# Two decoder stacks in one kernel: sums of squares taken as the residual is added, first weight splits moved ahead of the norm's transposes, separate last sums, and decay-mixer heads taken in pairs

## What is computed

```python
def rms_norm(x, g, eps=NORM_EPS):
    xf = x.astype(jnp.float32)
    y = xf * lax.rsqrt(jnp.mean(xf * xf, axis=-1, keepdims=True) + eps)
    return (y * g.astype(jnp.float32)).astype(x.dtype)

def swiglu_ffn(h, norm, w13, w2):
    u = rms_norm(h, norm) @ w13
    return (jax.nn.silu(u[..., :FFN_HIDDEN]) * u[..., FFN_HIDDEN:]) @ w2

def wkv7_scan(r, w, k, v, a, bb):          # the decay mixer: 8 heads of 64 columns
    ...
    def step(state, inp):
        r_t, w_t, k_t, v_t, a_t, b_t = inp
        sa = jnp.einsum("bhvk,bhk->bhv", state, a_t)
        state = state * w_t[:, :, None, :] + sa[..., None] * b_t[:, :, None, :] + v_t[..., None] * k_t[:, :, None, :]
        return state, jnp.einsum("bhvk,bhk->bhv", state, r_t)
```

## Time and profile before

| | us |
|---|---|
| median of 3 runs (lowest, highest) | 3027.68 (3025.43, 3028.09) |
| the profiled execution | 3027.91 |
| its span, first to last instruction | 3026.1 |
| PE busy | 2659.0 (88%) |
| DVE, ACT, POOL busy | 1861.2, 1412.3, 363.6 |
| `moe`, from its first expert matmul (2047.72) to the end | 978.4 |

### The profile page before, as it was taken

How to read it: one execution, slowest core, us unless ns; L and a number is a source line. 1 busy time by engine, 2 the same in 40 slices (tenths; PEclk the granted TensorE clock), 3 DMA queues, 4 the chain that set the end, 5 groups by cost and what they waited for, 6 DMA issues and landing times. The chain is left out here.

```text
span 3026.1 us, 37637 instructions
## 1 busy us (share of the span) xinstructions
PE 2659.0 (88%) x14146; PEld 2222.7 (73%) x14146; DVE 1861.2 (62%) x2377; ACT 1412.3 (47%) x1835; POOL 363.6 (12%) x241
## 2 busy tenths in 40 slices
PE   7788886998889789878898978659999999999998
PEld 6447664897887479755797957647888888888886
DVE  3653334554757444443453754457898898988987
ACT  3231112443554144312443431127777777777776
POOL 3101120001444000000000422220000000000000
PEclk9877778998999899986999978769999999999999
DMA  6600011554423055330554510038999999999996
GB/s 226 207 28 1 1 42 51 193 174 141 140 94 116 15 174 187 133 121 0 186 176 144 182 51 1 1 154 325 368 384 365 372 380 372 372 376 370 382 368 226
DMA packets 180226, 574.54 MB, mean 190 GB/s; under 512 B 10975, under 2 KB 80735, under 8 KB 136989
## 3 DMA queue, kind: packets, MB, share of 16 engines
q1 hardware_dynamic: 175884, 558.01, 50.0%
q0 software_dynamic: 3264, 11.80, 1.5%
q10 hardware_dynamic: 976, 3.33, 0.3%
HBM read 564.98 MB, written 6.29 MB: 189 GB/s over the span
## 5 line engine op out<-in xcount | busy, mean ns | idle before, releaser
L2851 DVE TENSOR_TENSOR moe_weights_low<-ring,moe_weights_high 128x1024 fp32r<-128x1024 f32 x672 | 782.4, 1218 | 109.4 <-ACT moe_weights_high L2806 107.0
L2806 ACT CAST moe_weights_high<-ring 128x1024 fp32r<-128x1024 f32 x672 | 685.8, 1051 | 106.1 <-PE banks L254 102.5
L252 PE MATMUL banks<-moe_weights_high,moe_rows_high 128*128 128x512 f32 x896 | 354.5, 396 | 2.5 <-DVE moe_rows_low L2836 2.5
L254 PE MATMUL banks<-moe_weights_low,moe_rows_high 128*128 128x512 f32 x896 | 350.1, 391 | 0.0
L253 PE MATMUL banks<-moe_weights_high,moe_rows_low 128*128 128x512 f32 x896 | 349.5, 390 | 0.0
L252 PE MATMUL banks<-ffn_x_high,ffn_weights_high 128*128 128x256 f32 x1056 | 300.1, 284 | 15.4 <-DVE ring_low L2405 15.4
L253 PE MATMUL banks<-ffn_x_high,ring_low 128*128 128x256 f32 x1056 | 299.6, 284 | 0.0
L254 PE MATMUL banks<-ffn_x_low,ffn_weights_high 128*128 128x256 f32 x1056 | 299.2, 283 | 0.0
L2405 DVE TENSOR_TENSOR ring_low<-ring,ffn_weights_high 128x2048 fp32r<-128x2048 f32 x66 | 148.0, 2288 | 137.6 <-ACT ffn_weights_high L2377 137.6
L252 PEld LDWEIGHTS banks<-ffn_x_high,ffn_weights_high 128*128 128x128 f32 x1056 | 202.6, 192 | 18.8 <-issue 16.4
L253 PEld LDWEIGHTS banks<-ffn_x_high,ring_low 128*128 128x128 f32 x1056 | 202.0, 191 | 2.3
(11 more groups left out here) (523 smaller groups left out, 5152.2 us busy)
## 6 DMA issues: line engine op xcount, KB each, us to landing
ring<-in_moe_gate_pieces SPq DMA_DIRECT2D x112, 1024.0 KB, 7.2
ring<-in_moe_up_pieces SPq DMA_DIRECT2D x112, 1024.0 KB, 7.4
ring<-in_moe_down_pieces SPq DMA_DIRECT2D x112, 1024.0 KB, 7.2
ring<-in_ffn_w SPq DMA_DIRECT2D x66, 1024.0 KB, 7.8
ring<-in_od_w_in SPq DMA_DIRECT2D x10, 2048.0 KB, 8.3
ring<-in_o_w_in SPq DMA_DIRECT2D x8, 2048.0 KB, 8.6
ring<-in_e_ffn_w_gate SPq DMA_DIRECT2D x11, 1024.0 KB, 5.5
ring<-in_e_ffn_w_up SPq DMA_DIRECT2D x11, 1024.0 KB, 8.1
```

What stands on the lines that cost most here:

```text
L252: pe.matmul(out_, lh, rh, start=start, stop=False)
L254: return pe.matmul(out_, lh, rl, start=False, stop=stop)
L2806: act.copy(hi[:, b * 1024:(b + 1) * 1024], piece).then_inc(sems["hi_done"], 1)
L2851: dve.tensor_tensor(lo[:, b], piece, hi[:, b].bitcast(F32), ALU.subtract).then_inc(sems["lo_done"], 1)
```

## The change

1. `sum_squares`: after every sum into `h` (a token tile and a half of the columns) ACT squares that 128x512 part with a row sum, scaled by 1/1024, into one of four columns. `rstd_of_h` then takes one DVE instruction and the same POOL power, and `scaled_h` scales in four 128x512 parts; the transposes of the first four column blocks wait for the first two parts alone. Nine norms take this way; that of `mix0` doesn't.
2. In the three feed-forwards the casts of the first up weights stand on ACT ahead of the transposes' evictions, the first subtraction on DVE ahead of L427's, the second behind. In `mamba` and `gdn` the splits of the narrow product and of two more pieces stand there (`early`). The projection before a feed-forward leaves the ring's first slot alone (`pass_over_first_slot`), and SP's first two loads of a feed-forward wait for that slot only. After a feed-forward each slot has a mark of its own, and the next load takes the third slot.
3. In a feed-forward's last body the split of the `down` weights comes behind the first step, not the second; the last step's four bank sums are finished and added one by one.
4. The decay mixer's heads go in pairs: four 128x128 transposes, one 128x512 copy, and the scores of the two heads from SBUF's two halves of partitions into two banks. The transposes of pair i+1 come ahead of the scores of pair i.

```diff
+        def sum_squares(t, half):
+
+            added = V.at()
+
+            @block.scalar
+            def _(act):
+                for due in unseen(act, S.at()):
+                    act.wait_ge(*due)
+                act.wait_ge(*added)
+                act.activation(squares[:], h[:, t, half * 512:(half + 1) * 512], ACT.Square, scale=D ** -0.5,
+                               accum_out=h_sums[:, t, half:half + 1]).then_inc(*S.tick())
+
+        def rstd_of_h():
...
+                dve.scalar_tensor_tensor(out=rstd, in0=h_sums[:, :, 0], scalar=EPS, in1=h_sums[:, :, 1], op0=ALU.add,
+                                         op1=ALU.add).then_inc(*V.tick())
+            return rstd, reciprocal_root(rstd, TT, V.at())
+
+        def scaled_h(scaled):
...
+                for half in range(2):
+                    c = slice(half * 512, (half + 1) * 512)
+                    for t in range(TT):
+                        dve.tensor_scalar(scaled[:, t, c], h[:, t, c], rstd[:, t:t + 1], None, ALU.mult).then_inc(*V.tick())
+                    marks.append(V.at())
+            return lambda k0: marks[k0 // 4]
...
+            def early():
+                few.append(split_few(w_in, INNER + CONV, NH))
+                for n in range(2):
+                    split_one(n)
+                for n in range(2):
+                    parts_ready[n] = split[n][2]()
+            after_rooms, top[0] = top[0], keep
+            normed = norm_turned(h, D, None, x_parts, g_in, params_landed, early)
...
+            @block.scalar
+            def _(act):
+                act.wait_ge(up_landed[0], 32)
+                for c in first_parts:
+                    act.copy(high[0][:, c], units[0][:, c]).then_inc(up_high, 1)
...
+            first_low(0)
+            normed = transpose_split(scaled, KD, scaled_ready, xh, xl, g, params_landed)
+            first_low(1)
...
             def _(sp):
-                for due in unseen(sp, ring_before):
+                for due in unseen(sp, ring_before[0]):
                     sp.wait_ge(*due)
...
                 up_columns(0, 0)
+                for due in unseen(sp, ring_before):
+                    sp.wait_ge(*due)
                 run(body, sp)
...
-                down(steps // 4, 1, stop=True)
+                pe.wait_ge(hl_done, steps)
+                for t in range(TT):
+                    for n in range(2):
+                        rows, cols = slice(t * P, (t + 1) * P), slice(n * 512, (n + 1) * 512)
+                        passes(pe, acc[t * 2 + n].ap, (hh[1][:, rows], hl[1][:, rows]),
+                               tuple(w[:, 1, cols] for w in down_w[0]), start=False, stop=True).then_inc(*M.tick())
+                        summed.append(M.at())
...
-                        if j % 2 == 1:
+                        if j % 2 == (1 if count == 4 else 0):
...
-            for s in slots:
-                s.free = (down_done, steps)
+            slots[0].free, slots[1].free, slots[2].free = (up_done, steps), M.at(), (down_done, steps - 2)
+            slot_turn[0] = 2
...
+                turn_pair(0)
+                for i in range(H // 2):
+                    if i + 1 < H // 2:
+                        turn_pair(i + 1)
+                    pair_scores(i)
...
+                    for j in range(4):
+                        for g in range(2):
+                            last = pe.matmul(two[g].ap[:, j * P:(j + 1) * P], tv[half[g], j, 256:384], tv[half[g], j, 0:P],
```

More of the change, by code:

```diff
@@ L332, in take_slot, with pass_over_first_slot @@
             return slots[(slot_turn[0] - 1) % SLOTS]
+        def pass_over_first_slot(loads):
+            turn, used = slot_turn[0], 0
+            while used < loads:
+                s = slots[turn % SLOTS]
+                turn += 1
+                if s.lent:
+                    continue
+                used += 1
+                if s is slots[0]:
+                    slot_turn[0], used = turn, 0
         def load_weights(src, shape3):
@@ L357, in _ @@
                 def _(pe):
-                    for due in unseen(pe, bank.free, ready):
+                    for due in unseen(pe, bank.free, ready(k0) if callable(ready) else ready):
                         pe.wait_ge(*due)
@@ new lines, in rwkv, with turn_pair, _ @@
+                groups = [dict(work[g], mv=work[g]["TTm"].rearrange("p (h n) -> p h n", h=4)) for g in range(2)]
+                copied = []
+                def turn_pair(i):
+                    c = slice(i * P, (i + 1) * P)
+                    bank = take_bank()
+                    @block.tensor
+                    def _(pe):
+                        for due in unseen(pe, bank.free, scaled):
+                            pe.wait_ge(*due)
+                        for m, x in enumerate((lr, k, kk, r)):
+                            last = pe.transpose(bank.ap[:, m * P:(m + 1) * P], x[:, t, c], ident)
+                        last.then_inc(*M.tick())
+                    turned = M.at()
+                    @block.scalar
+                    def _(act):
+                        for due in unseen(act, turned, idle[0], idle[1], scaled):
+                            act.wait_ge(*due)
+                        act.copy(tv[:, i, :], bank.ap).then_inc(*S.tick())
+                    bank.free = S.at()
+                    copied.append(S.at())
@@ new lines, in pair_scores, with _ @@
+                def pair_scores(i):
+                    one = [tv[half[g], i, :] for g in range(2)]
+                    two = [take_bank() for g in range(2)]
+                    @block.tensor
+                    def _(pe):
+                        for due in unseen(pe, two[0].free, two[1].free, copied[i]):
+                            pe.wait_ge(*due)
+                        for g in range(2):
+                            pe.matmul(two[g].ap[:, 0:256], one[g][:, 0:P], one[g][:, 256:512], start=True, stop=True)
+                        for g in range(2):
+                            pe.matmul(two[g].ap[:, 256:512], one[g][:, P:256], one[g][:, 256:512], start=True,
@@ L1375, in _ @@
                                       stop=True).then_inc(*M.tick())
-                        have = M.at()
+                    have = M.at()
+                    for g in range(2):
                         @block.vector
@@ L1591, in project_turned_parts, with product, _ @@
-            for later in behind[-2:]:
-                if later:
-                    later()
+            def early():
+                for i in range(2):
+                    split_one(i)
+                for i in range(2):
+                    parts_ready[i] = split[i][2]()
+            def product(w, first_col, n_tiles, ready, take):
+                behind = []
+                for i in range(1 - PIECES, 0):
+                    run_ahead(i, n_tiles, split_one, split, parts_ready)
+                for i in range(n_tiles):
+                    run_ahead(i, n_tiles, split_one, split, parts_ready)
+                    slot, _, low, _ = loaded[i // 4 * 4]
+                    high, at, _ = split[i]
+                    j = i % 4
+                    bank = take_bank()
+                    @block.tensor
+                    def _(pe):
+                        for due in unseen(pe, bank.free, ready, parts_ready[i]):
+                            pe.wait_ge(*due)
+                        for k in range(KD):
+                            last = passes(pe, bank.ap[:, 0:T], (high[:, k, :], low[:, k, j * P:(j + 1) * P]),
+                                          (x_high[:, k, :], x_low[:, k, :]), start=(k == 0), stop=(k == KD - 1))
+                        last.then_inc(*M.tick())
+                    piece_free[at] = slot.free = M.at()
+                    bank.free = take(i, bank.ap[:, 0:T], M.at())
+                    behind.append(after_take.pop() if after_take else None)
+                    if len(behind) > 2 and behind[-3]:
+                        behind[-3]()
+                for later in behind[-2:]:
+                    if later:
+                        later()
```

240 lines of the change are left out of this document (110 added, 130 removed).

## The result

| | us |
|---|---|
| before, median of 4 runs beside those of the change | 3027.06 (3025.43 to 3028.09) |
| changed kernel, median of 4 runs | 2934.61 (2932.58 to 2941.74) |
| ratio, 95% interval | 0.9699 (0.9682 to 0.9717) |
| forecast (range) | 2963.0 (2944 to 2975) |

By stages, from the end of the last sum into `h` to the next such end, the two profiled executions (spans 3026.1 and 2931.3) compare as follows. A term of the forecast is the sum of its parts that fall into the stage.

The account below looks back on a forecast made before the run. PE bounds the kernel, alone from `moe`'s first expert matmul and busy 88% before; savings 5.9+13.0+18.4+3.6+4.5+19.2 = 64.6 from 3027.9, less 0.2, give about 2963 us, range 2944 to 2975.

Parts of the forecast that it names:

- Part 5: Decay mixer's heads in pairs: saves 10.5 at t=1 and 12.1 at t=0, less 3.4 at the inversion, net 19.2 us.
- at 0.50 a pair is 0.99 + 3.94: Decay mixer's heads at half clock: transposes 0.99 plus as many scores as before 3.94, 4.93 us a pair.
- rival A: Decay mixer's scores: the two partition halves overlap, eight instructions in five steps, 9.3 more saved, 2954 us; chance 0.32.
- the -3.4 for `N`: Decay mixer: the inversion waits for all 3.62 of N, made for both groups in turn; loses 1.7 us each t.
- with the clock rising as well, 2944: Decay mixer's heads: overlap of the two halves plus a rising clock gives 2944 us instead of 2954.
- Part 1: Norms: squares beside the sums and scalings of 512 save 2.1 us at `cross0`, 1.2 at `moe`, sum 5.9.
- Part 2: Entry of the three feed-forwards: last sum to first product 9.4 us instead of 13.7, saving 4.35 each, 13.0.
- Part 3: Tail of the three feed-forwards: idle 2.7, half clock 1.6 and sums 1.85 saved, 6.15 us each, 18.4.
- Part 4: `mamba` and `gdn` entries: earlier narrow product and no gap before the following one, saving 3.6 and 4.5 us.
- B: Feed-forward, `mamba` and `gdn` entries: casts waiting for weights hold back evictions, 10.6 less saved, 2974 us; chance 0.15.
- C: Both inversions: half clock stays through 57 us that were at full clock, adding 57, 3020 us; chance 0.03.
- D: Entries of five stages: first weights each 14 us late, 71 in all, kernel slower at 3032 us; chance 0.02.

Follow-up runs that it names:

- copy_not_hidden: Changed kernel with a pair's transposes right ahead of its own scores, so PE idles for ACT's copy once a pair; 2946.98 us.
- same_half_busy_t1: single_heads_ahead with two added products of a constant block per head, in t=1's heads alone, from partitions 0 to 63, the heads' own half; 3012.34 us.
- other_half_busy_t1: single_heads_ahead with two added products of a constant block per head, in t=1's heads alone, from partitions 64 to 127, the other half; 2994.75 us.
- single_heads_ahead: Kernel before, heads still one by one from one half of the partitions, but the next head's transposes ahead of this one's scores; 3004.83 us.
- casts_behind: Changed kernel with the feed-forwards' first casts back behind the evictions and both first subtractions behind L441's; 2945.8 us.
- tail_as_before: Changed kernel with the feed-forward's end as before: last down split behind the second step, four sums behind the last product; 2966.37 us.
- only_pairs: Kernel before with the decay mixer's pairs of heads and nothing else of the change; 2973.97 us, ratio 0.9837.
- halves_not_in_turn: Changed kernel with the four score instructions of one half ahead of the other half's four, instead of two and two in turn; 2931.45 us.
- kept_busy_short_ffn: Changed kernel with unread constant-block products on PE at the feed-forwards' entries, two ahead of the norm's transposes and four behind; 2933.96 us, ratio 0.9688.

## Why the prediction was wrong, step by step

- **Part 5, wrong by 28.9.** It said 19.2, the stretch from t=0's first transposes to t=1's last state product gave 190.1 - 142.0 = 48.1. The heads gave 43.5 where 22.6 were forecast, and what lies behind them gave 4.6 where 3.4 were to be lost. Three terms failed. First, "at 0.50 a pair is 0.99 + 3.94": the eight score instructions run in four steps, not eight, nor five as rival A had it. At half clock a pair of `copy_not_hidden` has four instructions in 0.99, where the earlier trace rows has two in 0.98. Second, the clock: the rows of half clock were taken as a property of the heads, but in t=1 it stayed down as long as all scores used one half of the partitions and rose when both were in use (`same_half_busy_t1` against `other_half_busy_t1`); in t=0 it fell with idle and one half together, and held when either was gone (`single_heads_ahead`, `copy_not_hidden`). Pairs without idle hold full clock, or regain it. Third, the -3.4 for `N`: its products overlap as well and run at full clock, so the inversion starts 221.71 - 219.93 = 1.8 behind N's start, not 3.7 (2.0 in the earlier trace rows), and it is DVE's masks that it waits for. The largest part of the 4.6 is the clock once more: t=0's group products take 15.4 (from 262.55), 19.7 before (from 284.87 to 304.57, where the clock fell earlier). Of the 43.5 saved in the heads, `single_heads_ahead` shows what hiding the copy brings (14.7 in t=0, 6.8 in t=1). The rest, 6.3 and 15.7, is what pairs bring: in t=0, at full clock throughout, four sets of transposes less (some 0.55 each) and, the larger part, the overlap (0.97 for eight scores, not two times 1.05); in t=1 the clock as well.
- **Rival A had the mechanism, at 0.32, and too small a price.** What the Trainium skill says in "TensorE: Matmul & The Clock Gate", section "Part 3: Packing small matmuls — row/col tiling", that products in different row groups run at once, held for these f32 products (eight of both halves in 0.97, four of one half in 1.05); the forecast of 2963 went against it for want of a row. The "with the clock rising as well, 2944" added 10 for the clock, where it was worth more: at t=1 30.2 became 7.7.
- **Part 1, norm: 2.1 forecast, 1.9 measured** at `cross0` (3.1 against 5.0 behind *a*). `moe` was wrong in sign: the power came 0.3 later, not 1.2 earlier, since GpSimd's DMA issues wait for ACT's squares now, which the step did not follow through. It mattered for 1.3; 2.7 were the router's product at half clock, which comes and goes between kernels with the same `moe`: without it the entry gains 0.2 to 0.5. Of `cross0`'s 3.8, 1.9 are clock of that kind as well.
- **Part 2, entry: right**, 9.1 for 9.4, releaser as said, and `casts_behind` gives 2.7 back. Part 3, end: right, 18.4 forecast, 18.1 by `tail_as_before`. Part 4: `mamba` 4.2 for 3.6. In `gdn` 2.0 came up to the second product and 4.3 by some 120 PE instructions into the stage (30.5 behind *a* before, 26.2 now), for 4.5 forecast: right. The other 3.3 of the 7.6 are clock, which no step had: 32 transposes took 5.05, not 6.63, and `only_pairs`, with `gdn` as before, got 6.4 by such changes alone.
- **Rivals B, C and D** did not come. At `ffn0` ACT's casts started with no wait for a load, at 468.56. In `mamba` and `gdn` ACT did wait 1.9 and 1.6 for the load of the first pieces, which is B's mechanism, but the narrow products had DVE's L441 as releaser and not that. C's 57 us at full clock stand in no row: in the two inversions before the change the clock was at 1.00 for 37.6 and 37.5 us. D's 71 late would end at 3034, not 3032. Neither bears on the result.
- The range was too narrow at its low end. It took rival A with a little of the clock, but not the case in which all heads overlap at full clock, though both were named. From the forecast's own numbers, halved for the clock, that is 0.5 of transposes and four steps of 0.25, 1.5 a pair, 6 for a t.

## What to carry to other kernels

Where a product contracts over 64 rows, put its pairs into both halves of the partitions: the second was all but free here, in either of the two orders tried. Before a row at half clock goes into a sum, ask what PE did before it and whether the change alters that; a term at half clock has a second price at full clock, which belongs in the range. Where a sum into memory gets a new follower on another engine, look who at the next stage waits for that follower: here GpSimd's DMA issues. And before work of GpSimd goes beside a norm's scaling on DVE, look at how long the scaling takes there: 0.47 became 2.57 in `tail_as_before`.

## What was new about the chip

Never being idle did not bring the clock back while products used one half of the partitions alone (0.50 over 37.0 us with PE busy for all of it); with both halves it was back 2.4 us into the heads (291.21 less 288.78), with both halves but an idle of some 0.76 a pair only after 13. Work from the second half costs next to no time: 13.1 and 12.8 us for eight heads with and without it. A scaling on DVE that met a subtraction on GpSimd ended 0.28 behind it each time (0.94 and 2.57, not 0.47). The time that the first products behind a norm spend at half clock differs between kernels with the same code there (4.25 or 6.99 for the router's 32), so that one stage of one trace can be off by 2 to 3 us, `mix0` by up to 6.7 (404.7 to 411.4), and `gdn` by up to 8.8 (338.5 in `halves_not_in_turn`, 347.3 in `kept_busy_short_ffn`).
